# One round of four light experts moved from the twelfth place to the third, with halved loads for the first pair's slots

## The reference

```
h = h + mixed(h)                          # first half
hn = rmsnorm(h, norm_ffn_g)
gsel = argmax(hn @ w_rg + b_rg)           # 1 of 4 groups for each token
topv, topi = top_k(elog of that group, 2) # 2 of its 8 experts
combine = softmax(topv) * softmax(glog)[gsel]
for e in range(32):                       # gate, up: 1024 x 512, down: 512 x 1024
    y += combine[:, e] * (silu(hn @ w_gate[e]) * (hn @ w_up[e])) @ w_down[e]
out = rmsnorm(h + y, norm_final_g)
```

## Time and profile before

| | before |
|---|---|
| executions, median of 3 | 923.19 us |
| profiled execution, its own time | 926.1 us |
| its span | 924.4 us |
| TensorE busy | 876.0 us, 95% |
| VectorE, ScalarE busy | 47%, 23% |
| mean granted TensorE clock | 0.984 of full |
| DMA in the span | 246.85 MB, mean 267 GB/s |

### The profile page before, as it was taken

The page is one execution under the profiler, slowest core; times in us unless marked ns, Lnnn a source line. Parts: engine busy times, 40 slices in busy tenths (PEclk is TensorE's granted clock), DMA queues, the critical chain, the costliest instruction groups (busy, mean ns, idle before and its releaser), DMA issues.

```text
span 924.4 us, 11247 instructions
## 1 busy us (share of the span) xinstructions
PE 876.0 (95%) x4613; PEld 565.8 (61%) x4613; DVE 433.3 (47%) x805; ACT 214.7 (23%) x388; POOL 3.7 (0%) x15
## 2 busy tenths in 40 slices
PE   5999999999999999999999999999999999986595
PEld 4888888877777888888734545445445364452332
DVE  6528325677675344436786135342352433512213
ACT  5422222464444222223200111011010011010113
POOL 0000000000000100000000000000000000000000
PEclk9999999999999999999999999999999999998799
DMA  9343312121222653691389999999999999999994
GB/s 331 79 91 97 113 64 91 46 93 55 83 78 60 212 138 91 255 401 57 152 344 397 399 429 427 414 425 427 416 429 416 428 428 413 427 412 430 426 409 196
DMA packets 65286, 246.85 MB, mean 267 GB/s; under 512 B 21928, under 2 KB 45520, under 8 KB 52688
## 3 DMA queue, kind: packets, MB, share of 16 engines
q1 hardware_dynamic: 65152, 246.07, 68.0%
q10 hardware_dynamic: 80, 0.02, 0.0%
HBM read 243.98 MB, written 2.10 MB: 266 GB/s over the span
## 4 chain that ended last, share of the span: by engine, by line
PE 88%; DMA 5%; DVE 2%; ACT 1%; issue 1%; SPq 1%; DVEq 0%; ACTq 0%
PE bank L789 20%; PE bank L821 10%; PE bank L501 10%; PE bank L503 10%; PE bank L502 10%; PE bank L773 5%; DMA R<-w_down 4%; PE bank L528 3%; PE bank L529 3%; PE bank L530 3%; PE bank L848 2%; PE bank L849 2%; PE bank L588 1%; PE bank L610 1%; DMA raw<-w_in 1%
## 5 line engine op out<-in xcount | busy, mean ns | idle before, releaser
L789 PE MATMUL bank<-R,packT 128*64 128x512 f32 (+1 forms) x1024 | 199.9, 602 | 3.6 <-DMA R<-w_up 3.6
L789 PEld LDWEIGHTS bank<-R,packT 128*64 128x64 f32 (+1 forms) x1024 | 63.1, 131 | 124.1 <-issue 123.1
L1203 DVE TENSOR_TENSOR wlo<-raw,whi 128x2048 fp32r<-128x2048 f32 x33 | 75.5, 2287 | 85.5 <-ACT whi L969 85.5
L501 PE MATMUL bank<-xnT_hi,whi 128*128 128x512 f32 x288 | 113.7, 395 | 0.6 <-DVE wlo L1203 0.6
L503 PE MATMUL bank<-xnT_hi,wlo 128*128 128x512 f32 x288 | 112.2, 390 | 0.0
L502 PE MATMUL bank<-xnT_lo,whi 128*128 128x512 f32 x288 | 112.1, 389 | 0.0
L821 PE MATMUL bank<-R,actT 128*64 128x512 f32 (+1 forms) x448 | 95.4, 619 | 9.3 <-DMA R<-w_down 8.6
L969 ACT ACTIVATE whi<-raw 128x2048 fp32r<-128x2048 f32 x34 | 64.9, 1909 | 67.3 <-PE bank L503 38.7
L821 PEld LDWEIGHTS bank<-R,actT 128*64 128x64 f32 (+1 forms) x448 | 29.8, 137 | 68.1 <-issue 68.1
L1674 DVE TENSOR_TENSOR h_tok<-bank,h_tok 128x512 f32<-128x512 f32 x104 | 63.1, 674 | 1.0 <-PE bank L849 1.0
L1665 DVE SCALAR_TENSOR_TENSOR y_lo<-bank,small,y_hi 128x512 fp32r<-128x512 f32 x28 | 21.0, 751 | 89.8 <-ACT y_hi L1122 89.8
(11 more groups left out here) (285 smaller groups left out, 1186.4 us busy)
## 6 DMA issues: line engine op xcount, KB each, us to landing
R<-w_gate SPq DMA_DIRECT2D x32, 2048.0 KB, 13.3
R<-w_up SPq DMA_DIRECT2D x30, 2048.0 KB, 13.3
R<-w_down SPq DMA_DIRECT2D x28, 2048.0 KB, 14.9
raw<-w_in SPq DMA_DIRECT2D x18, 1024.0 KB, 5.0
raw<-w_in SPq DMA_DIRECT2D x16, 256.0 KB, 4.3
raw<-w_branch_a SPq DMA_DIRECT2D x4, 1024.0 KB, 5.0
raw<-w_branch_b SPq DMA_DIRECT2D x16, 256.0 KB, 4.3
raw<-w_out SPq DMA_DIRECT2D x4, 1024.0 KB, 7.9
```

The costliest lines, as they stand in the source:

```text
L501: pe.matmul(dst, hi_w, hi_x, start=start, stop=False)
L789: mm = pe.matmul(dst[s * w:(s + 1) * w, :], packT[:, c, odd * P + s * w:odd * P + (s + 1) * w], R[2 * slots[s // 2][0] + s % 2][:, c * DE: ...
L1203: dve.tensor_tensor(wlo[c % 2][:, :], raw[c % 2][:, :], whi[c % 2][:, :].bitcast(F32), ALU.subtract).then_inc(lo_split, 1)
```

## The change

- The order of rounds: a round of four light experts comes at place 2, the heavy pairs at places 3 to 12, the other round of four at place 13 as before. `experts_of` says so, SyncE's first expert index `r` is now a running sum, and `sort_experts` turns `place` into a position (`scan_a`): the four heavier of the light ones first, then the 20 heavy, then the last four. `final_rows` works out the first row of each expert from that position.
- Steps 4, 5 and 6 are loaded in halves: those that take the slots of round 0's gate, up and down weights. `up_half_done` comes from `project`; for down, `project_down` has a path of its own for round 0, which goes through the four parts of the weights once, for both halves of the output, and not once for each.
- `fill(n)`: a matmul of n columns into bank 3, which nobody reads; one of 512 columns ahead of round 0's `turn_rows`, one of 256 behind it.

```diff
@@ -56,6 +56,7 @@
     OV_ROW = ITERS * P
+    FIRST_LIGHT = LIGHT // 2
     assert ITERS % 2 == QUADS % 2 == OV_PAIRS % 4 == 0 and ITERS == LAST + 1
@@ -286,7 +287,8 @@
         ranks_read, first_onehot, first_weights = sem("ranks_read"), sem("first_onehot"), sem("first_weights")
-        ordered, gate_half_done = sem("ordered"), sem("gate_half_done")
+        ordered = sem("ordered")
+        gate_half_done, up_half_done, down_half_done = (sem(f"{name}_half_done") for name in ("gate", "up", "down"))
         last_loaded = [sem(f"last_loaded{c}") for c in range(3)]
@@ -314,7 +316,7 @@
         def experts_of(i):
-            return 4 if i >= QUADS else 2
+            return 4 if i in (FIXED // 2, LAST) else 2
@@ -326,7 +328,7 @@
             ks = [step_at[i, m, a] for a in range(experts_of(i) // 2)]
-            return [(k % 4, 32 * (k // 4) + (64 if k % 4 == 0 and k else 32)) for k in ks]
+            return [(k % 4, 32 * (k // 4) + (64 if k % 4 < 3 <= k else 32)) for k in ks]
@@ -408,8 +410,9 @@
             DONE = (main.gate_done, main.up_done, main.down_done)
+            HALF_DONE, HALVED = (gate_half_done, up_half_done, down_half_done), (4, 5, 6)
             for i in range(1, ITERS):
-                n_e, r = experts_of(i), 2 * i - FIXED
+                n_e, r = experts_of(i), sum(experts_of(j) for j in range(FIXED // 2, i))
                 if i == LAST:
@@ -417,8 +420,6 @@
                         sp.wait_ge(ordered, 1)
-                    if n_e == 4:
-                        r = HEAVY + 2 * (r - HEAVY)
                     chosen = [sp.value_load(order[0:1, r + s:r + s + 1], min_val=0, max_val=NE - 1) for s in range(n_e)]
@@ -426,13 +427,14 @@
                         i4, m4, _ = steps[k - 4]
-                        if k == 4:
-                            for half, done in enumerate((gate_half_done, main.gate_done)):
+                        if k in HALVED:
+                            for half, done in enumerate((HALF_DONE[m4], DONE[m4])):
+                                part = slice(half * 4 * DE, (half + 1) * 4 * DE)
                                 sp.wait_ge(done, 1)
                                 for s in range(2):
-                                    sp.dma_start(R[s][:, half * 4 * DE:(half + 1) * 4 * DE].rearrange("p (c n) -> p c n", n=DE),
-                                                 w[0, chosen[s]].rearrange("(p c) n -> p c n", p=P)[:, 4 * half:4 * half + 4, :]
-                                                 ).then_inc(slot_loaded[0], 16)
+                                    sp.dma_start(R[2 * (k % 4) + s][:, part].rearrange("p (a n) -> p a n", a=1),
+                                                 w[0, bass.ds(chosen[2 * a + s], 1), :, :].rearrange("a (p c) n -> p a (c n)", p=P)
+                                                 [:, :, part]).then_inc(slot_loaded[k % 4], 16)
                             continue
@@ -806,14 +808,27 @@
-            def project_down(line, slots, i, added):
+            def project_down(line, slots, i, added, half_done=None):
...
                 w = P // n_e
-                for n, done in enumerate((line.y_left, line.down_done)):
+                dones = line.y_left, line.down_done
+                if half_done is not None:
+                    for c in range(FT):
+                        for n in range(2):
+                            for s in range(n_e):
+                                mm = pe.matmul(bank[5 + n][s * w:(s + 1) * w, :], actT[:, c, s * w:(s + 1) * w],
+                                               R[2 * slots[0][0] + s][:, c * D + n * 512:c * D + (n + 1) * 512],
+                                               start=(c == 0), stop=(c == FT - 1))
+                            if c == FT - 1:
+                                mm.then_inc(dones[n], 1)
+                        if c == FT // 2 - 1:
+                            mm.then_inc(half_done, 1)
+                    return
+                for n, done in enumerate(dones):
                     if added is not None:
@@ -864,6 +879,10 @@
                           start=False, stop=True).then_inc(last_spread, 1)
+
+            def fill(n):
+
+                pe.matmul(bank[3][:, 0:n], ident[:, :], h_tok[:, 0, 0:n], start=True, stop=True)
@@ -876,16 +895,20 @@
                 turn_weights(main, odd)
-                project(main, slots_of(i, 1), odd, bank[1], main.up_done)
+                project(main, slots_of(i, 1), odd, bank[1], main.up_done, half_done=None if i else up_half_done)
                 if i:
                     spread(main, i - 1, 0, 1 - odd)
+                else:
+                    fill(512)
                 turn_rows(main, i)
+                if i == 0:
+                    fill(256)
                 if i:
...
                     pe.wait_ge(ranks_read, 1)
-                project_down(main, slots_of(i, 2), i, 8 * (i - 1) + 3 if i else None)
+                project_down(main, slots_of(i, 2), i, 8 * (i - 1) + 3 if i else None, None if i else down_half_done)
                 if odd:
@@ -1594,7 +1617,14 @@
                 then(dve.tensor_reduce(place[:, rest], sort_cmp[:, :, :], AX.X, ALU.add))
-                then(dve.tensor_tensor(order_cmp[:, :, :], place[0:1, rest].unsqueeze(1).to_broadcast([1, SORTED, SORTED]),
+                then(dve.tensor_scalar(scan_b[:, rest], place[:, rest], float(HEAVY), -float(HEAVY + FIRST_LIGHT),
+                                       ALU.is_ge, ALU.mult))
+                then(dve.scalar_tensor_tensor(out=scan_a[:, rest], in0=place[:, rest], scalar=float(FIRST_LIGHT),
+                                              in1=scan_b[:, rest], op0=ALU.add, op1=ALU.add))
+                then(dve.tensor_scalar(scan_b[:, rest], place[:, rest], float(HEAVY + FIRST_LIGHT), float(HEAVY),
+                                       ALU.is_ge, ALU.mult))
+                then(dve.tensor_tensor(scan_a[:, rest], scan_a[:, rest], scan_b[:, rest], ALU.add))
+                then(dve.tensor_tensor(order_cmp[:, :, :], scan_a[0:1, rest].unsqueeze(1).to_broadcast([1, SORTED, SORTED]),
                                        ov_iota[:, 0:SORTED].unsqueeze(2).to_broadcast([1, SORTED, SORTED]), ALU.is_equal))
@@ -1610,10 +1640,11 @@
                 then(dve.tensor_scalar(base_row[:, :], first_row[:, :], -2.0 * P, None, ALU.add))
-                then(dve.tensor_scalar(base_row[:, rest], place[:, rest], float(LIGHT_ROWS),
-                                       float(HEAVY * (ROWS - LIGHT_ROWS)), ALU.mult, ALU.add))
-                then(dve.tensor_scalar(delta[:, rest], place[:, rest], float(ROWS), None, ALU.mult))
-                then(dve.tensor_tensor(base_row[:, rest], base_row[:, rest], delta[:, rest], ALU.min))
+                then(dve.tensor_scalar(delta[:, rest], scan_a[:, rest], float(HEAVY + FIRST_LIGHT), -float(FIRST_LIGHT),
+                                       ALU.min, ALU.add))
+                then(dve.tensor_scalar(delta[:, rest], delta[:, rest], 0.0, float(ROWS - LIGHT_ROWS), ALU.max, ALU.mult))
+                then(dve.scalar_tensor_tensor(out=base_row[:, rest], in0=scan_a[:, rest], scalar=float(LIGHT_ROWS),
+                                              in1=delta[:, rest], op0=ALU.mult, op1=ALU.add))
...
                 then(dve.tensor_tensor(scan_a[:, :], scan_b[:, :], cap[:, :], ALU.add))
```

## The result

Five executions of the changed kernel took 927.94 us in the median (927.62 to 928.99), beside 923.19 for the kernel before (five, 922.73 to 927.80): ratio 1.0038, 95% interval 1.0020 to 1.0056, so slower by 0.2 to 0.6%. The forecast was +1.4 us and a time of 924.6. By the medians the change costs 4.7 us in the first comparison and 1.9 us in the second. Of the 2.9 us between the two, 1.9 come from the kernel before (923.19 in five executions, 925.08 in 35) and 1.0 from the changed one.

The account below looks back on a forecast made before the run. TensorE sets the end up to the last issue, the last 8.39 MB transfer after it. Round 0 -1.69, places 2 and 3 against 12 +4.09, last transfer -1.0: +1.4 on 923.19 gives 924.6 us, range 921.3 to 928.2.

Parts of the forecast that it names:

- Wait ahead of place 2's down: Light round at place 2: TensorE waits 11.7 us for the down weights; the projection then takes 8.68 us.
- Round 0: Fills in two waits of round 0 keep the clock up: down projection 7.09 us, not 8.78, gain 1.69 us.
- The halves: Loads of steps 4 to 6 in halves start sooner, but TensorE waits for none: worth 0, bounds 0 and 0.3.
- The move: Light round at place 2: waits at places 2 and 3 against those at place 12, +4.09 us.
- The end is set by TensorE up to the last issue and by that transfer: Place 13: TensorE sets the pace until the last weights are issued (forecast 886.8), then the last 8.39 MB transfer does.
- the rival that the stream sets the end: End of the kernel: the weight stream, not TensorE, sets it, so the new order pays in full: 915.5 us; 2 in 100.
- The last transfer: Last two steps at place 13, issued into an empty queue, take 1.0 us less, bounds 0 and 1.2.
- the 15.2 us behind the last part: From the start of the last matmuls to the span's end: 15.2 us that the change doesn't touch.
- The branch rival: Jump ahead of place 13: its 6.17 us may fall to 2.5 with fewer weights queued, 920.9 us; chance 0.09.
- The first rival: Round 0's gains don't show (926.3 us) or waits reach upper bounds; slower, 0.40 including the upper bounds singly.
- The likeliest case: Whole kernel: within 0.2% of no change, with either clock at place 3; 922.8 to 926.0 us, chance 0.46.
- the rival named for its upper end: No gain from round 0's fills, 926.3 us, with one addition at full, such as late landings adding 1.2.

Follow-up runs that it names:

- e1: Kernel before plus only the two fill matmuls of round 0: 924.21 us, ratio 0.9984 to the kernel before.
- e3: Changed kernel without fills and without the new halves, so only the light round moved to place 2: 927.96 us, ratio 1.0022 to the kernel before.
- e2: Kernel before plus only the loads of steps 4, 5 and 6 in halves: 925.94 us, ratio 1.0001 to the kernel before.
- e4: Changed kernel with the light round at place 6 instead of 2: 928.20 us, ratio 1.0018 to the kernel before.
- e7: Changed kernel with the first part of the last down weights issued after half of place 13's gate projection: 921.54 us, ratio 0.9962 to the kernel before.
- e9: Kernel before, old order, plus round 0's fills and last down weights issued after half of place 13's gate projection: 924.41 us, ratio 0.9994 to the kernel before.
- e11: Old order with round 0's fills, the early last issue and nine fills ahead of the branch: 925.25 us, ratio 0.9991 to the kernel before.
- e5: Changed kernel itself run again, 12 executions beside 35 of the kernel before (the second comparison): 926.94 us against 925.08, ratio 1.0014.
- e6: Changed kernel plus fills ahead of place 3's up projection and in the last down projection's waits: 924.27 us, ratio 0.9988 to the kernel before.

## Why the prediction was right, step by step

With 1.58 us added to the changed kernel's times:

| step | forecast | trace |
|---|---|---|
| down projection of round 0 | 7.09 | 7.09 |
| issue of place 2's first down step | 525.4 | 525.4 |
| down of place 2 starts, takes | 549.1, 8.68 | 549.2, 8.58 |
| gate of place 3 starts | 558.9 | 558.9 |
| up of place 3 starts, takes | 568.6, 8.77 | 568.6, 8.78 |
| down of place 12 ends | 861.3 | 861.1 |
| last issue | 886.8 | 886.9 |
| issue to last part | 23.75 | 24.0 |
| last part to the end of the span | 15.2 | 16.6 |

- **Wait ahead of place 2's down**: 10.8 us, not 11.7, since 1.0 us of waiting came earlier, ahead of the up projection. The start of the down projection is set by the landing and is the one forecast.
- **Round 0**: 1.69 forecast, 1.7 measured alone (e1). That the two agree so well is luck: e1's interval goes from 0.1 to 2.9 us, and e3's trace has no fall of the clock there without any fill.
- **The halves** cost or give nothing that e2 can tell (-1.6 to +1.7 us), in the old order, where TensorE waits for none of these loads. In the new order the traces put place 2's down projection 2.2 us sooner with them than without (e3). The forecast had this within its landing times and not as a gain of the halves.
- **The move** costs by its hand-over. A light round frees two slot pairs at once, its down weights come 24 us later, and the next round's gate and up weights after them. At place 12 the spreading, the branch and `final_g`'s matmuls, 18 us, lie behind it, and cover that; at places 2 and 6 a heavy round stands there and waits. e4 has the four waits at places 6 and 7 too, behind a queue that was not empty, so of the reasons that I named the empty queue isn't needed. e3 puts the move, without the new halves, at +2.1 us (0.6 to 3.5), my 3.1 in it.
- **The end is set by TensorE up to the last issue and by that transfer.** e7 shows it: an issue after half of the gate projection instead of the whole brings 5.4 us in the median. That excludes, for the changed kernel, the rival that the stream sets the end. e9 and e11 show that in the old order the same issue brings nothing, since the stream is still full then. So the new order does buy the stream 5 us of slack, as one would hope of it; the change had nothing that used them.
- **The last transfer** gave 0.7 of the 1.0 in the first trace, 0.5 in e5's.
- **What I missed** is the last term: I took the 15.2 us behind the last part as untouched. In both traces of the changed kernel the last part ran at the lower clock, 1.5 us more, and the stretch behind its start is 16.6 us. The waits before it (0.33 and 3.10 us) are those of before (0.35 and 3.06), where it didn't. It took 3.5 to 3.6 in all four traces of the new order with the late issue (the changed kernel, e3, e4, e5), and 1.92 in the three of the old order with it (before, e1, e2), but 3.28 and 3.35 in e9 and e11, also of the old order. So among the traces with the late issue it goes with the order, but e9 and e11 show that the order isn't the whole of it. Why stays open.
- **The branch rival** fell: 6.29 us beside 6.17, with 12 us of weights queued ahead of it where there were 22. Over all traces it takes 6.17 to 6.69 us in the five of the old order and 5.99 to 6.60 in the eight of the new one, nowhere near the 3.4 or 2.5 of the rival. The Trainium skill ("Runtime: NRT & Kernel Launch", section "Instruction fetch mechanics") says that a taken branch out of the fetched window waits for a DMA fetch of its target; no run here shows whether this branch does. A stall that shrinks with the queued weights was my inference from it, and no trace has one.
- **The first rival** (no gain from the fills in the usual execution) was half right in its reason, that the clock doesn't fall in each execution, and wrong in its result.
- **The size** was met less well than the steps. Counted from the first load of the expert stage, the rest of the span is 3.1 us longer in the changed kernel's trace and 3.6 in e5's, for a forecast of 1.4; the stretch behind the last part is 1.4 of the difference. The likeliest case, less than 0.2% apart, is at its edge in the second comparison (1.9 us) and not what the first one shows (4.7 us). That the first comparison's 927.94 lies inside the stated 921.3 to 928.2 also owes something to the way the range was written: the rival named for its upper end comes to 926.3 + 1.2 = 927.5, and the branch rival named for its lower end to 920.9. The stream's end, 568.4 + 32 x 9.8, is 882.0 and not 881.7, which changes nothing in the result.

## What to carry to other kernels

In this kernel a stream of loads and an engine are nearly balanced. Moving a load-heavy stage forward gave the stream 5 us of slack, and paid only with a second edit that spends that slack, an earlier last issue (0.9962 with both, 0.9994 for the early issue without the move, 1.0014 for the change without it). The light round was cheapest at place 12, in front of 18 us of work that doesn't need the next weights, and cost about the same at places 2 and 6 (1.0014 and 1.0018). Fills that keep the clock up gained where the engine's own path set the end (e6) and nothing where the stream did (e11), and must be counted anew when an earlier edit shortens the wait that covers them.

## What the runs showed that I had not expected

The same short wait lowers TensorE's clock in one execution and not in another: after 2.0 us ahead of an up projection it took 8.78 us in the changed kernel and e5 and 7.09 in e3, e4 and e7, and after 1.20 and 0.73 us in round 0 the down projection took 8.78 us before and 7.09 in e3. So one trace can't price such a wait. The executions of an unchanged kernel spread accordingly: 35 of the kernel before, beside e1 to e4, took 922.21 to 928.92 us, the five with a mean clock of 0.981 or less 928.0 in the mean, the four at 0.987 923.9. A median over five of them can be off by 2 us: the first comparison's 923.19 stands beside 925.07 to 925.89 in the three larger sets.
